# Two attentions of a diffusion block: a stage of their own, or woven head pair by head pair with linear layers

## The chip, the cores and the metric

One core of one Trainium2 chip runs the whole program. The metric is the device time of one execution in microseconds; the kernel before took 3308.38 us (median of three runs, 3305.70 to 3311.96). The core has a matrix engine (PE, with its weight loads shown as PEld), a vector engine (DVE), a scalar engine (ACT), a general one (POOL) and a queue engine (SP) that issues most transfers. Each runs its own list of instructions in order and waits for the others by semaphores. PE alone multiplies matrices; its sums land in PSUM and are read from there by DVE or ACT.

## The reference, cut to what matters

The program is a small diffusion transformer in fp32: two layers on 512 latent and 256 context tokens, width 1024, then a third block. The change concerns layer 0. Its mixer runs a window attention (8 query heads of width 64, 2 key heads, blocks of 128 queries, keys of the block before, its own and the next one, and all 256 context keys), an attention of the context tokens on themselves, and beside them a gated linear recurrence (HGRN, 4 heads, two directions).

```python
def window_attention(q, k, v, k_ctx, v_ctx, sink):
    ...
    def block(i):
        qb = lax.dynamic_slice_in_dim(q, start, ATTN_BLOCK, axis=3)
        kb = lax.dynamic_slice_in_dim(kp, start, span, axis=2)
        s_lat = jnp.einsum('bkgqd,bksd->bkgqs', qb, kb) * scale
        s_lat = jnp.where(valid, s_lat, -jnp.inf)
        s_ctx = jnp.einsum('bkgqd,bkcd->bkgqc', qb, k_ctx) * scale
        p = jax.nn.softmax(jnp.concatenate([sink_col, s_lat, s_ctx], axis=-1), axis=-1)
        return p_lat @ v  +  p_ctx @ v_ctx           # two einsums

def first_block(...):
    m_lat = jnp.split((cond_lat @ mod_w[layer] + mod_b[layer])[:, None, :], 6, axis=-1)
    h_lat = modulate(rms_norm(x, norm_g[layer, 0]), m_lat[0], m_lat[1])
    y_ctx, y_lat = even_mixer(h_ctx, h_lat, even_w_in[j], even_w_out[j], ...)
    # even_mixer: p = split_parts(h_lat @ w_in); attention on a_q, a_k, a_v; recurrence on b_*
```

## The kernel before, in words

Every linear is summed in three passes: weights are split into a rounded `hi` part (ACT, a CAST) and a remainder `lo` (POOL), inputs likewise, and PE sums hi x hi, lo x hi and hi x lo. A weight tile of 128x2048 comes by a DMA of SP into one of two `stage` buffers. `linear` runs one layer as a stage of its own; `chain` yields the same work piece by piece, and `Woven(...).upto(place)` lets another loop pull it in up to a place. Places are counted in matmuls of 512 columns: a job such as `bf1` (forget gates of head 1) or `bqg1` (query and output gate) or `bi0` (inputs of heads 0 and 1) has 72 of them. Stages are blocks with a barrier of all engines at both ends.

Layer 0 runs in this order. (1) First loads, the norm of x with its modulation, and the linears `aq` and `akv`. The modulation vectors are sums on DVE over tiles of 512 KB (`sum_up`, L926: two sums for each of 24 tiles, in four buffers); `first_mods` makes the two tiles of a chunk of the norm, `norm_split` calls it for chunks 0 and 1 ahead of the root and for chunk c+2 behind chunk c. (2) Norm and rotation of the attention's q and k, woven with `bf0`, `bqg0`, `bi0`. (3) `attend("win", ...)`: 4 blocks of 8 heads. Per head PE makes the scores of 640 keys against `q_zero` (full height, with the other key head's half filled with zeros), DVE scales and masks them and takes the maximum, ACT exponentiates, PE transposes 5 blocks, ACT copies them, PE multiplies by the values; per block of 8 heads DVE divides and PE transposes back. Nothing else runs there. (4) `attend("ctxa", ...)`: the same with 256 keys, 2 blocks. (5) The HGRN recurrence, 8 jobs (head and direction), woven with `bf1`, `bqg1`, `bf2`, `bqg2`, `bi1`, `bf3`, `bqg3` (504 places); `begin_of` says at which place each job starts, and jobs 6 and 7 run behind the linears. Much later, in layer 1, the linear `rg` has 24 modulation sums beside it (`rest_of_layer_1`), through two buffers.

## Time and profile before

| | us |
|---|---|
| median of three runs | 3308.38 |
| the profiled execution | 3308.32 |
| its span, first to last instruction | 3306.5 |
| PE busy | 2964.5 (90%) |
| DVE / ACT / POOL busy | 1268.1 / 1000.6 / 996.8 |
| loads from memory | 264.42 MB, 81 GB/s over the span |

A busy PE is an engine that had work under way, and its waits are put down to the instruction that released it. The stages above lie at 0 to 157.6 us, 157.6 to 233.6, 236.4 to 341.1, 341.1 to 370.4 and 370.4 to 633.3 us.

### The profile page before, as it was taken

To read this page: it belongs to the slowest core of one execution; us is meant where nothing else is said; L and a number is where in the kernel's file an instruction comes from. 1 tells how busy PE (TensorE), PEld (TensorE's weight loads), DVE (VectorE), ACT (ScalarE), POOL (GpSimd) and SP (SyncE) were. 2 spreads that over 40 slices of the span, in tenths; PEclk is the share of its full clock that TensorE was granted. 3 is DMA by queue.
4 is the path that set the end of the run, shared out by engine and by line. 5 is a ranking of instruction groups with operands and counts; after the bars stand their busy time and mean duration, and the time that the engine had idled before them with its cause. 6 is when DMAs were issued, how large, how long until landed. Compare 5 with 4: busy or idle time off the path is not lost. (4 is left out here: it accounts for less than half of the span.)

```text
span 3306.5 us, 38877 instructions
## 1 busy us (share of the span) xinstructions
PE 2964.5 (90%) x15588; PEld 2407.3 (73%) x15588; DVE 1268.1 (38%) x1869; ACT 1000.6 (30%) x1471; POOL 996.8 (30%) x482
## 2 busy tenths in 40 slices
PE   2789888679999999889997898999899999999998
PEld 1678787558888888868744686788668777886686
DVE  7456555472145116132015606511163554203523
ACT  2235554213211211422103314222243333324432
POOL 0220232112223222634102233344244433342333
PEclk7899899689999999999998999999989999999999
DMA  5300110141133113422202424432211111021121
GB/s 194 107 26 1 45 39 14 77 140 51 59 128 125 63 61 137 140 83 89 80 10 100 181 89 171 153 109 81 85 57 46 39 39 39 26 102 58 48 93 64
DMA packets 48958, 268.52 MB, mean 81 GB/s; under 512 B 5552, under 2 KB 6832, under 8 KB 28592
## 3 DMA queue, kind: packets, MB, share of 16 engines
q1 hardware_dynamic: 48816, 266.54, 23.0%
q8 instruction: 100, 1.64, 0.2%
q14 instruction: 42, 0.34, 0.0%
HBM read 264.42 MB, written 2.10 MB: 81 GB/s over the span
## 5 line engine op out<-in xcount | busy, mean ns | idle before, releaser
L416 POOL TENSOR_TENSOR shared_w_lo<-stage,shared_w_hi 128x2048 fp32r<-128x2048 f32 (+1 forms) x127 | 554.3, 4365 | 1363.1 <-ACT shared_w_hi L389 1360.0
L557 POOL TENSOR_TENSOR shared_w_lo<-stage,shared_w_hi 128x512 fp32r<-128x512 f32 (+2 forms) x233 | 300.7, 1319 | 515.6 <-ACT shared_w_hi L549 513.9
L389 ACT CAST shared_w_hi<-stage 128x2048 fp32r<-128x2048 f32 (+1 forms) x127 | 224.5, 1768 | 506.8 <-PE f0o_acc L479 134.5
L479 PE MATMUL f0i_acc<-norm_b_hi,shared_w_hi 128*128 128x512 f32 (+1 forms) x672 | 174.2, 341 | 2.0 <-PEq L368 2.0
L479 PE MATMUL f0i_acc<-norm_b_lo,shared_w_hi 128*128 128x512 f32 (+1 forms) x672 | 172.2, 337 | 0.0
L624 PE MATMUL two_acc<-norm_f_hi,shared_w_hi 128*128 128x512 f32 (+1 forms) x312 | 131.8, 422 | 9.1 <-DVE norm_f_lo L727 9.1
L549 ACT CAST shared_w_hi<-stage 128x1024 fp32r<-128x1024 f32 (+2 forms) x117 | 114.6, 1022 | 82.5 <-PE last_acc L624 43.9
L819 DVE TENSOR_TENSOR ffn_hidden<-f0i_acc,ffn_gate 128x512 f32<-128x512 f32 (+1 forms) x44 | 22.5, 553 | 301.0 <-PE f0i_acc L479 293.3
L479 PE MATMUL f1i_acc<-norm_e_hi,shared_w_hi 128*128 128x512 f32 x336 | 131.0, 390 | 2.3 <-PEq L368 1.6
L809 ACT CAST ffn_hi<-ffn_hidden 128x768 f32 (+3 forms) x44 | 32.0, 728 | 329.8 <-DVE ffn_hidden L819 329.8
L479 PE MATMUL f1i_acc<-norm_e_lo,shared_w_hi 128*128 128x512 f32 x336 | 130.8, 389 | 0.0
L624 PE MATMUL two_acc<-norm_f_lo,shared_w_hi 128*128 128x512 f32 (+1 forms) x312 | 129.9, 416 | 0.6 <-DVE dn_g_cum L2521 0.6
L479 PE MATMUL f0i_acc<-norm_b_hi,shared_w_lo 128*128 128x512 f32 (+1 forms) x672 | 124.5, 338 | 0.0
L479 PEld LDWEIGHTS f0i_acc<-norm_b_hi,shared_w_hi 128*128 128x128 f32 x672 | 102.7, 189 | 17.3 <-issue 2.3
L479 PEld LDWEIGHTS f0i_acc<-norm_b_lo,shared_w_hi 128*128 128x128 f32 x672 | 103.5, 189 | 15.6
L479 PEld LDWEIGHTS f0i_acc<-norm_b_hi,shared_w_lo 128*128 128x128 f32 x672 | 102.3, 188 | 15.1
L624 PE MATMUL last_acc<-norm_f_hi,shared_w_hi 128*128 128x512 f32 x256 | 102.6, 401 | 2.7 <-PEq L2431 1.8
L624 PE MATMUL last_acc<-norm_f_lo,shared_w_hi 128*128 128x512 f32 x256 | 102.0, 399 | 0.0
L479 PE MATMUL f0o_acc<-ffn_hi,shared_w_hi 128*128 128x512 f32 x352 | 92.2, 343 | 6.9 <-PEq L368 6.9
L624 PE MATMUL two_acc<-norm_f_hi,shared_w_lo 128*128 128x512 f32 (+1 forms) x312 | 92.1, 421 | 3.9 <-POOL shared_w_lo L557 3.9
L2206 DVE TENSOR_TENSOR ret_decayed<-ret_p_scores,ret_decay 128x512 f32<-128x512 f32 x24 | 16.5, 691 | 200.2 <-PE ret_p_scores L2179 100.8
L2646 POOL TENSOR_TENSOR delta_join<-delta_low,levels 128x512 f32<-128x512 f32 x56 | 72.4, 1303 | 65.7 <-PE delta_p L2688 38.4
(588 smaller groups left out, 7044.4 us busy)
## 6 DMA issues: line engine op xcount, KB each, us to landing
stage<-in_w_f0i SPq DMA_DIRECT2D x22, 1024.0 KB, 4.9
stage<-in_w_f1i SPq DMA_DIRECT2D x22, 1024.0 KB, 4.8
stage<-in_w_rv SPq DMA_DIRECT2D x16, 1024.0 KB, 4.8
mod_slots_a<-in_w_mod SPq DMA_DIRECT2D x24, 512.0 KB, 4.8
stage<-in_w_rqk SPq DMA_DIRECT2D x12, 1024.0 KB, 4.9
mod_slots_f<-in_w_mod SPq DMA_DIRECT2D x24, 512.0 KB, 4.0
mod_slots_e<-in_w_mod SPq DMA_DIRECT2D x24, 512.0 KB, 5.4
stage<-in_w_dqkv SPq DMA_DIRECT2D x12, 1024.0 KB, 4.9
```

The lines of the kernel that those rows point to most:

```text
L389: nc.scalar.copy(w_hi[:, slot, 0:size], stage[:, slot, 0:size]).then_inc(hi_ready, 1)
L416: nc.gpsimd.tensor_tensor(w_lo[:, slot, 0:size], stage[:, slot, 0:size], w_hi[:, slot, 0:size].bitcast(F32), ALU.subtract)\
L479: mm = nc.tensor.matmul(out[0:min(P, nt), b, 0:m], w[:, k, unit[1]:unit[1] + min(P, nt)], x[:, k, s:s + m], start=begin, stop=end)
L549: last = nc.scalar.copy(w_hi[:, index % 2, part], stage[:, index % 2, part])
L557: last = nc.gpsimd.tensor_tensor(w_lo[:, index % 2, part], stage[:, index % 2, part], w_hi[:, index % 2, part].bitcast(F32), ALU.subtract)
L624: mm = nc.tensor.matmul(out[0:min(P, nt), 0:m], weights[:, k, unit[1]:unit[1] + min(P, nt)], x[:, k, s:s + m], start=begin, stop=last)
L809: nc.scalar.copy(h_hi[:, bass.ds(t, 1), :], hidden[:].rearrange("p (o n) -> p o n", o=1))\
L819: last = nc.vector.tensor_tensor(hidden[:, s:s + m], res[1][:, b, 0:m], gate[:, s:s + m], ALU.mult)
L2206: nc.vector.tensor_tensor(decayed[:, n % 3, :], p_scores[:, n % 2, :], table[:, h % 2, at:at + LAT], ALU.mult).then_inc(rs["decayed"], 1)
L2646: nc.gpsimd.tensor_tensor(chunks(join[a][:]), chunks(low[a][:]), over_chunks(levels[:, m, :]), ALU.mult).then_inc(d["join"], 1)
```

## The change

`attend` is gone. One stage holds both attentions, unrolled into 24 pairs of heads (one head of each key head; 16 pairs of the window attention, 8 of the context's), woven with `bi0`, `bf1` and `bqg1`; the head-norm stage keeps `bf0` and `bqg0`, and the HGRN stage `bi1` and heads 2 and 3 (360 places). Queries and keys are used at half height (64 rows) without zeros; the keys are `k_rot` without padding, so that blocks 0 and 3 have 4 key blocks and not 5. The probabilities are divided before they are transposed, and the values are the stationary side, 64 columns wide, so that nothing is turned back. Each pair's scores are made one pair ahead. `begin_of` is new. In the first stage two modulation tiles are asked for ahead of x, the other twelve ahead of the next weight tile, chunks 0 to 3 are summed ahead of the root, and the first CAST stands behind the squares. Beside `rg` stand three sums per tile in place of four on six tiles.

```diff
-                        scales(dve, 0)
-                        scales(dve, 1)
+        SCALES_AHEAD = 4
+                        for c in range(SCALES_AHEAD):
+                            scales(dve, c)
 ...
-            return made["beside"]([0] * 8, [4] * 6 + [0, 0], scale_ffn_1)
+            return made["beside"]([0] * 8, [3] * 8, scale_ffn_1)
 ...
+                first_mod["load"](sp, 0)
+                first_mod["load"](sp, 1)
                 sp.dma_start(ones[:], io["ones"]).then_inc(loaded, 16)
                 sp.dma_start(x_lat[:], io["x"]).then_inc(loaded, 16)
 ...
-        def attend(tag, blocks, heads, q_copies, out_copies, width, kb_max, cols_out, scale, lse=None):
 ...
+            line_w = chain([input_job(0)] + head_jobs(1), acc_w, ahead=True)
+            weights_of = [2 if m < 16 else 1 for m in range(PAIRS)] + [1, 1]
 ...
+                    def scores(m):                       # PE
+                        i, c = divmod(m, 4)
+                        wait(pe, aw["scores_read"], 2 * m)
 ...
+                            for g in range(2):
+                                product(p_scores[g][:, 0:last - first], g, first, last)
+                            product(p_ctx[:, 0:CTX], 0, LAT, TOK).then_inc(aw["lat_scores"], 1)
+                            pe.wait_ge(aw["lat_scores"], m + 1)
+                            product(p_ctx[:, CTX:2 * CTX], 1, LAT, TOK).then_inc(aw["scores"], 2)
 ...
+                    scores(0)
+                    for m in range(PAIRS + 2):
+                        more.upto(pair_place(m))
+                        if m + 1 < PAIRS:
+                            scores(m + 1)
+                        if 1 <= m <= PAIRS:
+                            turn(2 * m - 2)
+                            more.upto((pair_place(m) + pair_place(m + 1)) / 2)
+                            turn(2 * m - 1)
+                        if m >= 2:
+                            mix_values(m - 2)
+                    more.rest()
 ...
+                    for m in range(PAIRS + 1):           # DVE
+                        for g in range(2):
+                            if m < PAIRS:
+                                read_scores(2 * m + g)
+                        more.upto(pair_place(m))
+                        for g in range(2):
+                            if m >= 1:
+                                normalize(2 * m - 2 + g)
+                        for g in range(2):
+                            if m < PAIRS:
+                                maximum(2 * m + g)
 ...
+                    for m in range(PAIRS + 2):           # ACT
+                        if 1 <= m <= PAIRS:
+                            copy_turned(2 * m - 2)
+                            copy_turned(2 * m - 1)
+                        if m < PAIRS:
+                            exponent(2 * m)
+                            exponent(2 * m + 1)
+                        if m >= 2:
+                            copy_out(m - 2)
+                        more.upto(pair_place(m))
 ...
-            line0 = chain(head_jobs(1) + head_jobs(2) + head_jobs(3), acc1, ahead=True)
+            line0 = chain([input_job(1)] + head_jobs(2) + head_jobs(3), acc1, ahead=True)
-            begin_of = [60, 130, 200, start_of["bqg2"][0] + 54, start_of["bf3"][0] + 2, start_of["bqg3"][0] + 10] + [after] * 3
+            begin_of = [56, 100, 160, start_of["bqg2"][0] + 56, start_of["bf3"][0] + 24, start_of["bqg3"][0] + 22] + [after] * 3
```

On PE, inside the window attention, this stood before: one head after the other, and nothing between (`turned` are the transposes, `mixed` the products with the values).

```order
L1167 MATMUL win_p_scores<-k_pad,q_zero 128x384
L1167 MATMUL win_p_scores<-k_pad,q_zero 128x256
L1176 MATMUL win_p_turned<-ident,win_row 128x128 x5
L1188 MATMUL win_p_mixed<-v_pad,win_probs 128x64 x5
L1167 MATMUL win_p_scores<-k_pad,q_zero 128x384
L1167 MATMUL win_p_scores<-k_pad,q_zero 128x256
```

And this stands there now, for one pair of heads (L630 are the sums of the linear `bf1`):

```order
L1408 MATMUL attend_scores<-k_rot,qk 128x384 x2
L1408 MATMUL attend_ctx_scores<-k_rot,qk 128x256 x2
L1428 MATMUL attend_turned<-ident,attend_row 128x128 x5
L630 MATMUL attend_acc<-norm_a_lo,shared_w_hi 128x384
L630 MATMUL attend_acc<-norm_a_hi,shared_w_hi 128x384
L630 MATMUL attend_acc<-norm_a_lo,shared_w_hi 128x384
L630 MATMUL attend_acc<-norm_a_hi,shared_w_hi 128x384
L630 MATMUL attend_acc<-norm_a_lo,shared_w_hi 128x384
L630 MATMUL attend_acc<-norm_a_hi,shared_w_hi 128x384
L1428 MATMUL attend_turned<-ident,attend_row 128x128 x5
L1439 MATMUL attend_mixed<-attend_probs,v_att 64x128 x10
```

The scores in it are those of the next pair, the transposes those of this pair and the products with the values those of the pair before; some six to eight matmuls of a linear stand at each of two places.

On DVE, at the same place of the program, one pair of heads is now this (`hgrn_i` is the reading of a sum of `bi0`); before, each head was the mask, the scaling, the sink column and the maximum, and the division came once in 8 heads:

```order
L1471 SCALAR_TENSOR_TENSOR attend_row<-attend_scores,window 128x384 [waits attend_turned,attend_scores]
L1474 TENSOR_SCALAR attend_row<-attend_ctx_scores 128x256
L1476 COPY attend_row<-small 128x1
L1210 COPY hgrn_i_980<-attend_acc 128x256 [waits unit_summed]
L1486 RECIPROCAL attend_inverse<-attend_total 128x1 [waits attend_exp]
L1490 TENSOR_SCALAR attend_row<-attend_row,attend_inverse 128x640 [waits attend_reciprocal]
L1486 RECIPROCAL attend_inverse<-attend_total 128x1 [waits attend_exp]
L1490 TENSOR_SCALAR attend_row<-attend_row,attend_inverse 128x640 [waits attend_reciprocal]
L1481 TENSOR_REDUCE attend_minus_max<-attend_row 128x1 [waits attend_scores_read] x2
```

The division works on the pair before, so that it stands between the reading and the maxima of this one, and the reading of a linear's sum stands ahead of both.

## Rows read from the trace of the kernel before

**Rows 1.** Busy time by stage: us, PE, PEld, DVE, ACT, POOL, clock, DMA share, GB/s
```profile
0.00:157.60 157.60, 80.21 (x416) 65.22 (x416) 93.05 (x145) 35.10 (x57) 18.82 (x8) 0.82 0.42 151
157.60:233.60 76.00, 67.47 (x366) 60.35 (x366) 41.44 (x36) 24.72 (x34) 28.38 (x26) 0.93 0.12 42
236.40:341.10 104.70, 94.77 (x624) 79.20 (x624) 59.51 (x136) 57.92 (x109) 0.00 (x0) 0.96 0.00 1
341.10:370.40 29.30, 23.89 (x136) 18.69 (x136) 16.02 (x52) 17.62 (x54) 0.00 (x0) 0.85 0.00 1
370.40:565.00 194.60, 169.94 (x1339) 158.69 (x1340) 106.31 (x160) 95.22 (x121) 65.22 (x42) 0.95 0.12 41
565.00:633.30 68.30, 37.23 (x280) 30.40 (x278) 31.94 (x45) 15.49 (x23) 3.57 (x2) 0.59 0.00 1
```

**Rows 2.** The same columns for the first transfers
```profile
4.00:24.00 20.00, 0.00 (x0) 0.00 (x0) 7.58 (x13) 3.61 (x2) 0.00 (x0) 1.00 1.00 413
```

**Rows 3.** DVE in order of time: start us, us, engine, line, op, count [idle before]
```profile
16.13 1.29 DVE L926 CUSTOM_DVE_ANT_0 mod_product_a<-mod_slots_a,conds_a,small 128x1024 f32<-128x1024 f32 x1 [16.13 <-DMA mod_slots_a<-in_w_mod]
...
24.92 5.26 DVE L926 CUSTOM_DVE_ANT_0 mod_product_a<-mod_slots_a,conds_a,small 128x1024 f32<-128x1024 f32 x1
...
38.35 4.95 DVE L721 RECIPROCAL norm_rstd<-norm_rstd 128x768 f32<-128x768 f32 x1 [6.36 <-ACT norm_rstd L694]
...
82.37 0.74 DVE L739 SCALAR_TENSOR_TENSOR norm_squares<-x_lat_in,scale_of,norm_rstd 128x512 f32<-128x512 f32 x1
...
90.39 0.74 DVE L739 SCALAR_TENSOR_TENSOR norm_squares<-x_lat_in,scale_of,norm_rstd 128x512 f32<-128x512 f32 x1
```

**Rows 4.** Group by form, head-norm stage: busy us, mean ns, idle before
```profile
L624 PE MATMUL head_acc<-norm_a_hi,shared_w_hi 128*128 128x384 f32 x64 | 24.0, 374 | 15.5 <-PEq L368 10.3 <-DVEq L1365 4.1 <-DVEq L1385 1.1
```

**Rows 5.** PE in order of time, one head of the window attention
```profile
274.61 1.30 PE L1167 MATMUL win_p_scores<-k_pad,q_zero 128*128 x4
275.74 0.71 PE L1176 MATMUL win_p_turned<-ident,win_row 128*128 128x128 f32 x5
276.29 1.23 PE L1188 MATMUL win_p_mixed<-v_pad,win_probs 128*128 x10
```

**Rows 6.** Groups by form, window attention (32 heads)
```profile
L1242 DVE TENSOR_REDUCE win_minus_max<-win_row 128x1 f32<-128x641 f32 x32 | 26.3, 821 | 1.1
...
L1236 DVE SCALAR_TENSOR_TENSOR win_row<-win_p_scores,window 128x384 f32<-128x384 f32 x32 | 17.6, 550 | 0.0
L1233 DVE TENSOR_SCALAR win_row<-win_p_scores 128x256 f32<-128x256 f32 x32 | 13.3, 416 | 0.0
```

**Rows 7.** DVE in order of time, a TENSOR_SCALAR in memory of 768 columns
```profile
374.18 0.68 DVE L1775 TENSOR_SCALAR hgrn_forget<-hgrn_forget,hgrn_bound 128x768 f32<-128x768 f32 x1 [5.31 <-DMA hgrn_restart<-in_restart]
```

**Rows 8.** PE in order of time, HGRN products at the end of the linears
```profile
568.74 0.66 PE L2007 MATMUL hgrn_p_out<-hgrn_scores,hgrn_i 128*128 128x128 f32 x4
...
571.34 0.87 PE L1979 MATMUL hgrn_p_scores<-hgrn_q_ref,hgrn_k_ref 128*32 128x64 f32 x48
572.14 1.16 PE L1994 MATMUL hgrn_p_kv<-hgrn_i,hgrn_k_end_tok 64*128 64x128 f32 x16
```

**Rows 9.** PE in order of time, half-height products and the linear behind them
```profile
423.76 0.71 PE L1994 MATMUL hgrn_p_kv<-hgrn_i,hgrn_k_end_tok 64*128 64x128 f32 x6
424.40 0.45 PE L624 MATMUL hgrn_acc<-norm_a_lo,shared_w_hi 128*128 128x384 f32 x1
424.68 0.34 PE L624 MATMUL hgrn_acc<-norm_a_hi,shared_w_hi 128*128 128x384 f32 x1
...
425.90 0.33 PE L624 MATMUL hgrn_acc<-norm_a_lo,shared_w_hi 128*128 128x384 f32 x1
```

**Rows 10.** Waits of PE from 370.4 to 633.3: us in total, times, longest
```profile
PE hgrn_p_scores L1979 <- DVE hgrn_q_cum L1796: 8.4, 5, 2.6
```

**Rows 11.** Queue of SP in order of time, the rg linear
```profile
1829.49 13.33 SPq L910 DMA_DIRECT2D mod_slots_f<-in_w_mod  x4
...
1843.98 13.29 SPq L910 DMA_DIRECT2D mod_slots_f<-in_w_mod  x4
```

More of the change, by code:

```diff
@@ L389, in round_hi @@
                             nc.scalar.copy(w_hi[:, slot, 0:size], stage[:, slot, 0:size]).then_inc(hi_ready, 1)
-                        if not begun:
-                            round_hi(0, 0)
-                        if made:
-                            made["act"](act)
+                        if side is not None and "sp_first" in side:
+                            made["act"](act, lambda: round_hi(0, 0))
+                        else:
+                            if not begun:
+                                round_hi(0, 0)
+                            if made:
+                                made["act"](act)
                         def body(t, j, last):
```

334 lines of the change are left out of this document (126 added, 208 removed).

## The prediction, as put on record before the change was run

> **What bounds the kernel now.** I read the table by stage first, then each stage's order of time, then groups and waits. The profiled execution took 3308.32 us, its span 3306.5, so 1.8 us lie outside it; the median of the runs is 3308.38, and sums made against the profile hold for it without correction. The table [rows 1] shows which stages a weave can fill. In the window attention PE is busy 94.77 of 104.7 us, in the context's 23.89 of 29.3, in the HGRN stage 169.94 of 194.6 as long as it has linears, then 37.23 of 68.3. So PE is the bound nearly everywhere in layer 0, also in the attentions, where DVE has 59.5 and ACT 57.9 us of 104.7. Hiding linears in PE's idle time alone can win some 15 us there. A larger gain has to come from less work of PE, so I count PE's work per pair of heads. The first stage is another case: PE 80 of 157.6 us, and DVE sets the pace with its modulation sums.
>
> **First stage.** Transfers run at 413 GB/s [rows 2]. Ahead of the first modulation tile stood x, context and ones, 3.2 MB or 7.8 us, which now come behind; the first sum moves from 16.1 us [rows 3] to about 8.4. But DVE has 16 sums to make now ahead of the root, 1.45 us each with their read-out, and only 4 buffers. Tile 4 is queued behind 8.7 MB and lands at about 26 us; the 8 sums on tiles 4 to 7 then last to 38. POOL's subtraction for the first weight tile, now later, falls among them. One sum took 5.26 us in place of 1.29 [rows 3], which costs 4 us and did before, so the reciprocal starts at 42 and not at 38.35. That the root itself is ready 6 us sooner, its CAST being gone from ahead of the squares, is then worth nothing. Behind it two chunks fewer carry sums: 52.0 us from the reciprocal to chunk 6 (38.35 to 90.39) less 2 x 5.8 is 40.4, so chunk 6 at 82.4 in place of 90.4. Eight us, of which I keep 7, as PE closes up over the last chunks. Bounds: 0 if the transfers queue worse, -12 if POOL's stall falls into a wait. The weight tile of `akv`, asked for behind all twelve loads now, is needed only 40 us later.
>
> **Head-norm stage.** `bi0` goes: 72 places. A place costs 0.232 us: seven matmuls of 384 columns in 1.22 us are 0.174 each, by 512/384 [rows 9]. That is 16.7 us. The chain of reciprocals on DVE (4.95 us each for 768 columns, as the one in [rows 3]; 5 chunks, with the rest of a chunk about 7.3 us) is 37 us long and fits into the remaining 59. PE waited 5.2 us for DVE's readings here, 10.3 more at the start [rows 4]. What gets worse is the end: silu of `bqg0` on ACT, a table load and two passes over 768 columns, some 3 us, stood beside `bi0` and now stands ahead of the barrier. Taken: -15, bounds -20 and -8.
>
> **Attention stage.** It replaces 136.8 us (233.6 to 370.4) and takes in 216 places, 50.1 us. PE's price of a pair of heads, five key blocks:
> - Scores. A head cost 1.13 us for 640 columns [rows 5], two cost 2.26. Half-height products may run side by side. The trace has such: 16 instructions of half-height 128 columns took 1.16 us, against 0.66 for only 4 at full height, 0.073 and 0.165 us each [rows 8]. The two masked parts then cost 1.1 us, and the two context parts, the second of which waits for the first, 0.9 with a wait of 0.1, less an overlap of 0.2 and rounded down: 1.8.
> - Transposes as before, 2 x 0.55 [rows 5].
> - Values. 1.23 us busy per head became 20 instructions of 128 columns in two column halves; at 0.073 that is 1.45, at the closer packing of the 128x32 products, 48 in 0.87 us [rows 8], far less. Taken: 1.3 for the pair.
> - Changes of form. Six half-height instructions took 0.71 us, and the first linear matmul behind them stood 0.28 us before the next, where 0.174 is usual [rows 9]: about 0.1 us a change, four a pair: 0.4.
> Sum 4.6, and 10.3 places of linears, 2.4: 7.0 us. Blocks 0 and 3 have four key blocks: scores 1.5, transposes 0.9, values 1.05, changes 0.4, linears 2.4: 6.25. DVE has per head 0.82 + 0.55 + 0.42 [rows 6], 0.15 for the sink, 0.3 for a reciprocal with its wait and 0.57 for the division (0.68 for 768 columns [rows 7]), 2.8, or 5.6 to 6.0 a pair with readings of sums. ACT has 57.92 / 32 = 1.8 a head [rows 1]. Both stay under 7.0, and the loop transpose, copy, exponential, division, transpose (0.55 + 0.7 + 1.0 + 0.9) has 4 us of other PE work beside it. A context pair is 3.3 us on PE and 3.6 on DVE, so 3.6. In all 8 x 7.0 + 8 x 6.25 + 8 x 3.6 = 135, 4 for the first pair, in which nothing overlaps, and 5 for the last two with the silu behind: 144, or +7 against 136.8, with 50 us of linears in it. Bounds: -10 (no price for the changes, context pairs PE-bound, no end) and +45. The latter is PE without anything side by side: 2.26 + 1.1 + 2.2 + 0.4 + 2.4 = 8.4, 7.3 and 4.3 a pair, 160 us, with the same ends and 10 of table loads and POOL against DVE.
>
> The half-height row is the nearest to the scores, so I go by it. The Trainium skill, TensorEngine Tiling (Array Packing), section Tiling Modes, says that changing the tiling mode drains the engine, which speaks against this change: 24 pairs go four times from one form to another. The trace shows a price of about 0.1 us for such a change [rows 9], 10 us in all; a full drain of the 0.3 us that one matmul takes there would make it 29 and the total about 3283. The same page, Restrictions and Gotchas, says that row tiles can't write the same PSUM bank at once, which would be why the second context part waits. No row here has that wait.
>
> **HGRN stage.** 144 places leave: -33.4 us. The eight jobs stay, and those inside the linears stand 44, 60, 40, 40, 70 and 64 places apart instead of 70, 70, 70, 92, 80 and 76. A job has 9 us of places and 8 to 11 of its own matmuls at 40, against some 11.5 us on DVE and in every second job 7 more for its norm. That is level with PE, and PE waited for the scaled queries 5 times already [rows 10]. I give back 8: -25, bounds -33 and -5. The tail of 68.3 us [rows 1] stays.
>
> **Beside rg.** Loads and sums of four modulation tiles held the queue 14.49 us (1829.49 to 1843.98 [rows 11]), with the next weight tile behind them; PE needs 48 x 0.232 = 11.1 a tile. Three take 10.9. Six tiles lost up to 3.4 each, 20 in all; I take half, as the first come early and the last two caught up. At the end three sums now stand behind the last reading, 5 to 6 us: -4, bounds -10 and +3.
>
> **Sum.** -7 - 15 + 7 - 25 - 4 = -44: 3308.3 - 44 = 3264.
>
> **Rivals.** (A) PE's halves don't run side by side between full-height work. Attention +45 in place of +7 less the 10 of contention: 3293 to 3302, say 3297. Against it stand the HGRN rows, which are taken between linears. (B) HGRN jobs are too dense. DVE's order (exponents of the next job ahead of this one's mask, the norm ahead of the next queries) makes PE wait in each of the six intervals by 4 more: -5 in that stage, 3284. For it: DVE would be 18.5 of 20 us busy at 40 places. (C) Slower: lock-step of the pairs. If scores, reading, division, maximum, exponential and transposes of a pair follow one another, since PE's linears stand in order behind a blocked transpose, a window pair takes 1.8 + 2.2 + 1.8 + 1.6 + 2.0 + 1.2 = 10.6, a context pair 5.5: 170 + 44 + 9 = 223 us, +86, and the total is 3343. It decides from about 188 us for the stage, 8.9 us a window pair. Against it: scores come a pair ahead, and rows have four slots. (D) Nothing moves: the linears taken in cost there what they cost before and PE's waits only change places, 3305. That needs A and B together.
>
> **How the numbers follow.** Forecast 0.66, B 0.13, A 0.12, D 0.03, C 0.06. Within the forecast the terms leave +-20. The range 3234 to 3298 holds the forecast, B and half of A. A measurement tells 0.2%, 6.6 us. Faster: forecast, B and nearly all of A, 0.91; same 0.03; slower 0.06.
>
> **What would show it.** The stage with the attentions lasts about 144 us, PE over 90% busy; a window pair comes every 7 us; the two scores' instructions of a pair start beside each other and one pair's take 1.8 us. The head-norm stage lasts 61 us, the HGRN stage up to its last linear 170, chunk 6 of the first norm starts at 82, `rg` is 4 us shorter. Window pairs above 8.9 us, or waits of PE for the division, would prove me wrong.

## The result and the profile after

The changed kernel took 3269.23 us (median of four runs, 3262.18 to 3279.86), the kernel before in the same runs 3309.64; the ratio is 0.9888, with a 95% interval of 0.9858 to 0.9918, about 37 us less. The forecast was 3264, the range 3234 to 3298. The profiled execution is the fastest of the four, 3262.18 us with a span of 3260.4. It is set against the span of 3306.5 before, 46 us less.

The page's line of busy times: PE's busy time is 36 us less in all (2964.5 before). 22.5 us of it lie in the stages of layer 0 (the windows below against those of the kernel before), where score products and products with values now use half the array each, two at a time. Another 7.6 lie beside `rg`, where the same matmuls ran at a higher granted clock (told under `rg_old`).

```profile
PE 2928.1 (90%) x15516; PEld 2363.9 (73%) x15516; DVE 1280.6 (39%) x1952; ACT 989.3 (30%) x1478; POOL 991.1 (30%) x478
```

The table of the windows by stage, to be read against [rows 1] (us, then busy us and instructions of PE, PEld, DVE, ACT and POOL, clock, DMA share, GB/s). A stage here begins with its first matmul; the attention stage is cut where the context's pairs begin, at 316.7.

```profile
0.00:148.50 148.50, 77.95 (x416) 63.61 (x417) 93.31 (x146) 35.22 (x58) 18.72 (x8) 0.83 0.44 160
148.50:209.40 60.90, 48.75 (x224) 41.41 (x224) 39.35 (x30) 23.01 (x33) 22.59 (x18) 0.91 0.10 35
209.40:316.70 107.30, 103.70 (x752) 80.77 (x752) 72.86 (x196) 48.16 (x106) 10.24 (x8) 0.95 0.09 30
316.70:364.60 47.90, 40.46 (x276) 28.16 (x275) 25.40 (x91) 28.55 (x76) 4.96 (x4) 0.92 0.00 1
364.60:533.00 168.40, 141.84 (x1134) 130.18 (x1134) 95.24 (x149) 83.84 (x111) 51.47 (x34) 0.90 0.10 35
533.00:607.40 74.40, 38.30 (x290) 31.61 (x290) 36.38 (x51) 19.12 (x28) 3.58 (x2) 0.63 0.02 5
```

With the same bounds the kernel before has 157.9, 79.9, 132.9, 191.5 and 73.5 us. What has to be seen: the head-norm stage lasts 60.9; the window part of the attention stage has PE busy 103.7 of 107.3 us; the context part of it is the poorer one, 40.5 of 47.9; the HGRN stage up to the last linear is 23 us shorter; its tail is as long as ever. The rest of the program follows with the same lengths, but for `rg` (122.6 us between the first matmuls of `rg` and `ro` before, 109.7 now) and about 5 us in later parts whose code is unchanged.

One window pair on PE, in order of time (pair 12, 256 masked columns; the `acc` rows are `bqg1`):

```profile
289.46 0.70 PE L1408 MATMUL attend_scores<-k_rot,qk 64*128 64x256 f32 x4
290.00 0.59 PE L1408 MATMUL attend_ctx_scores<-k_rot,qk 64*128 64x256 f32 x2
290.74 0.67 PE L1408 MATMUL attend_ctx_scores<-k_rot,qk 64*128 64x256 f32 x2
291.34 0.77 PE L1428 MATMUL attend_turned<-ident,attend_row 128*128 128x128 f32 x5
291.86 0.42 PE L630 MATMUL attend_acc<-norm_a_lo,shared_w_hi 128*128 128x384 f32 x1
292.12 0.34 PE L630 MATMUL attend_acc<-norm_a_hi,shared_w_hi 128*128 128x384 f32 x1
...
293.17 0.71 PE L1428 MATMUL attend_turned<-ident,attend_row 128*128 128x128 f32 x5
293.80 1.31 PE L1439 MATMUL attend_mixed<-attend_probs,v_att 128*64 128x128 f32 x20
295.05 0.44 PE L630 MATMUL attend_acc<-norm_a_hi,shared_w_hi 128*128 128x384 f32 x1
295.33 0.34 PE L630 MATMUL attend_acc<-norm_a_lo,shared_w_hi 128*128 128x384 f32 x1
```

The group of scores lasts 1.88 us (289.46 to 291.34). The four instructions of both masked parts, x4 in one row, start in twos 0.01 us apart, one of each head, and take 0.54 us up to the next row. One head's 256 columns alone would be 0.45, by the 1.13 us for 640 in [rows 5]: the two heads run side by side. The second context product starts 0.74 behind the first, though its own columns are 0.45; 0.3 is the wait for the first. Twenty products with the values take 1.25 us, what ten took for one head. The first linear matmul behind transposes or values stands 0.26 to 0.28 before the next, where 0.17 is usual [rows 9]; how much of that is a change of form is told in the section after the experiments.

The start of the context part, ACT first, then PE:

```profile
321.86 1.28 ACT L1182 ACT_TABLE_LOAD   x1
323.15 1.49 ACT L1182 ACTIVATE hgrn_forget<-hgrn_forget 128x1536 f32<-128x1536 f32 x1
324.55 1.97 ACT L555 CAST shared_w_hi<-stage 128x1024 fp32r<-128x1024 f32 x2
326.42 0.58 ACT L1520 COPY attend_probs<-attend_turned 128x512 f32<-128x512 f32 x1
```

```profile
327.15 1.08 PE L1428 MATMUL attend_turned<-ident,attend_row 128*128 128x128 f32 x4 [3.05 <-ACT attend_probs L1520]
328.16 1.98 PE L1439 MATMUL attend_mixed<-attend_probs,v_att 128*64 128x128 f32 x16
```

ACT loads the table for the sigmoid of `bf1`, works through 1536 columns, rounds a weight tile (`CAST`) and only then copies the transposed probabilities that PE's next transposes wait for. PE stands 3.05 us; the transposes behind take 1.0 where 0.5 is usual, since the granted clock is at the lower of its two levels (0.5, 1.2 GHz) for some 6 us from there. This pair lasts 9.6 us; in a run below where the stall is gone it lasts 5.0.

### The profile page after: what moved, and what is told of

Its sections match the earlier page's. It is cut to its first block and busy times, and to the rows that moved or that the text cites. A ratio compares the mean times of both kernels' runs of the same rounds, so it can differ in the third digit from the quotient of the medians.

```text
span 3260.4 us, 38562 instructions
## 1 busy us (share of the span) xinstructions
PE 2928.1 (90%) x15516; PEld 2363.9 (73%) x15516; DVE 1280.6 (39%) x1952; ACT 989.3 (30%) x1478; POOL 991.1 (30%) x478
## 5 line engine op out<-in xcount | busy, mean ns | idle before, releaser
L630 PE MATMUL two_acc<-norm_f_hi,shared_w_hi 128*128 128x512 f32 (+1 forms) x312 | 131.8, 422 | 9.1 <-DVE norm_f_lo L736 9.1
L828 DVE TENSOR_TENSOR ffn_hidden<-f0i_acc,ffn_gate 128x512 f32<-128x512 f32 (+1 forms) x44 | 22.5, 553 | 296.1 <-PE f0i_acc L485 288.5
L630 PE MATMUL two_acc<-norm_f_lo,shared_w_hi 128*128 128x512 f32 (+1 forms) x312 | 130.0, 417 | 0.6 <-DVE dn_g_cum L2465 0.6
L485 PEld LDWEIGHTS f0i_acc<-norm_b_hi,shared_w_lo 128*128 128x128 f32 x672 | 101.9, 188 | 14.6
L630 PE MATMUL last_acc<-norm_f_hi,shared_w_hi 128*128 128x512 f32 x256 | 102.6, 401 | 2.7 <-PEq L2375 1.8
L630 PE MATMUL last_acc<-norm_f_lo,shared_w_hi 128*128 128x512 f32 x256 | 102.0, 399 | 0.0
L630 PE MATMUL two_acc<-norm_f_hi,shared_w_lo 128*128 128x512 f32 (+1 forms) x312 | 90.6, 415 | 4.0 <-POOL shared_w_lo L563 4.0
L485 PE MATMUL f0o_acc<-ffn_lo,shared_w_hi 128*128 128x512 f32 x352 | 92.5, 344 | 0.0
```

What stands on the lines that cost most here:

```text
L485: mm = nc.tensor.matmul(out[0:min(P, nt), b, 0:m], w[:, k, unit[1]:unit[1] + min(P, nt)], x[:, k, s:s + m], start=begin, stop=end)
L630: mm = nc.tensor.matmul(out[0:min(P, nt), 0:m], weights[:, k, unit[1]:unit[1] + min(P, nt)], x[:, k, s:s + m], start=begin, stop=last)
L828: last = nc.vector.tensor_tensor(hidden[:, s:s + m], res[1][:, b, 0:m], gate[:, s:s + m], ALU.mult)
```

## The experiments

Stage lengths are between first matmuls. "Attention" goes from the first score product to the first linear of the HGRN stage; before, with both attentions and without linears, it was 132.9. Ratios are to the kernel before, with 95% intervals; `again`, `crossed`, `serial` and `apart` ran on one chip, `banked`, `sig_early`, `rg_old` and `b_first` on one, `sig_late`, `best` and `hg_wide` on one, `split` by itself.

| run | median us | before there | ratio | attention us |
|---|---|---|---|---|
| again | 3270.62 | 3300.21 | 0.9889 (0.9848 to 0.9930) | 154.1 |
| crossed | 3254.01 | 3300.21 | 0.9845 (0.9814 to 0.9877) | 145.0 |
| serial | 3299.78 | 3300.21 | 0.9989 (0.9972 to 1.0006) | 180.8 |
| apart | 3298.18 | 3300.21 | 0.9992 (0.9972 to 1.0013) | 179.2 |
| banked | 3253.32 | 3311.72 | 0.9824 (0.9804 to 0.9845) | 142.9 |
| sig_early | 3266.90 | 3311.72 | 0.9856 (0.9837 to 0.9876) | 152.8 |
| rg_old | 3285.68 | 3311.72 | 0.9913 (0.9893 to 0.9932) | 154.1 |
| b_first | 3299.36 | 3311.72 | 0.9959 (0.9937 to 0.9980) | 132.8 |
| sig_late | 3250.85 | 3302.68 | 0.9852 (0.9809 to 0.9896) | 140.0 |
| best | 3261.38 | 3302.68 | 0.9872 (0.9845 to 0.9899) | 140.0 |
| hg_wide | 3272.70 | 3302.68 | 0.9911 (0.9884 to 0.9938) | 154.1 |
| split | 3254.89 | 3306.71 | 0.9831 (0.9805 to 0.9858) | 138.2 |

**again.** The changed kernel, no edit.

> The changed kernel once more, nothing edited, as the base on the same chip for the runs beside it. Its first runs lay between 3262 and 3280 us. If the stages in the trace come out within 1 us of the first trace (148.5, 60.9, 155.2 and 242.8 us for the first, head-norm, attention and HGRN stages), differences of the stages between traces of a few us are real, and the spread of the totals comes from elsewhere.

Measured: stages of 148.5, 61.8, 154.1 and 248.5 us. The first three agree within 1.1, but the HGRN stage doesn't: its tail lasted 80.3 us against 74.4. So a difference of 2 us can be read from a trace up to the last linear of HGRN, while the totals spread by 20 us (3257 to 3277 here). What the tail does is told at the end.

**crossed.**

```diff
-                            for g in range(2):
-                                product(p_scores[g][:, 0:last - first], g, first, last)
-                            product(p_ctx[:, 0:CTX], 0, LAT, TOK).then_inc(aw["lat_scores"], 1)
-                            pe.wait_ge(aw["lat_scores"], m + 1)
-                            product(p_ctx[:, CTX:2 * CTX], 1, LAT, TOK).then_inc(aw["scores"], 2)
+                            product(p_scores[0][:, 0:last - first], 0, first, last)
+                            product(p_ctx[:, CTX:2 * CTX], 1, LAT, TOK).then_inc(aw["lat_scores"], 1)
+                            product(p_scores[1][:, 0:last - first], 1, first, last).then_inc(aw["scores"], 1)
+                            pe.wait_ge(aw["lat_scores"], m + 1)
+                            product(p_ctx[:, 0:CTX], 0, LAT, TOK).then_inc(aw["scores"], 1)
```

> Changed kernel, but the four score products of a window pair are issued crossed: masked part of head 0, context part of head 1, masked part of head 1, context part of head 0, with the wait on the first context part ahead of the last product. Theory (products on different row halves run side by side, if they go to different PSUM banks): both halves have 640 columns, so that the group takes 1.1 to 1.3 us in place of 1.88 to 2.09, about 0.8 us less a window pair, 16 pairs, attention stage 155 to about 143 us and the total 10 to 12 us less. Rival (halves don't run side by side; the 1.88 is something else): the group stays at 1.9 to 2.3 us and the stage at 155.

Measured: the group takes 1.61 us in blocks 1 and 2 and 1.40 in blocks 0 and 3, 0.48 less each. PE in order of time, the group of pair 12:

```profile
283.47 0.48 PE L1408 MATMUL attend_scores<-k_rot,qk 64*128 64x256 f32 x1
283.48 0.48 PE L1408 MATMUL attend_ctx_scores<-k_rot,qk 64*128 64x256 f32 x1
283.79 0.38 PE L1408 MATMUL attend_scores<-k_rot,qk 64*128 64x256 f32 x1
283.80 0.38 PE L1408 MATMUL attend_ctx_scores<-k_rot,qk 64*128 64x256 f32 x1
284.01 0.59 PE L1408 MATMUL attend_scores<-k_rot,qk 64*128 64x256 f32 x2
284.24 0.70 PE L1408 MATMUL attend_ctx_scores<-k_rot,qk 64*128 64x256 f32 x2
284.87 0.77 PE L1428 MATMUL attend_turned<-ident,attend_row 128*128 128x128 f32 x5
```

Each product is two instructions. Those of the first two products start in twos, one of each head, 0.01 us apart. Of the last two products only one instruction of each runs beside the other: the context product of head 0 starts 0.23 us behind the masked one of head 1. The attention stage lost 9 to 10 us (the theory had 12), the total 16, so that the halves do run side by side; the rival would have left the group as it was. The group did not come down to the 1.1 to 1.3 of the theory: the wait still stands in it.

**serial.**

```diff
-                            for g in range(2):
-                                product(p_scores[g][:, 0:last - first], g, first, last)
-                            product(p_ctx[:, 0:CTX], 0, LAT, TOK).then_inc(aw["lat_scores"], 1)
-                            pe.wait_ge(aw["lat_scores"], m + 1)
+                            product(p_scores[0][:, 0:last - first], 0, first, last).then_inc(aw["lat_scores"], 1)
+                            pe.wait_ge(aw["lat_scores"], 3 * m + 1)
 ...
```

> Changed kernel with a wait for the end of each score product ahead of the next one in the window pairs, so that nothing of them can run side by side. Theory (side by side): the group takes 2 x 1.13 us plus three waits of about 0.1, some 2.5 to 2.7 in place of 1.88 to 2.09; 16 pairs, the stage is 9 to 12 us longer and so is the total. Rival (nothing ran side by side before): only the two more waits are paid, 0.2 us a pair, stage and total +3.

Measured: 2.95 and 3.38 us a group. PE in order of time, the same kind of pair as above:

```profile
309.29 1.45 PE L1408 MATMUL attend_scores<-k_rot,qk 64*128 64x256 f32 x4
310.80 1.51 PE L1408 MATMUL attend_ctx_scores<-k_rot,qk 64*128 64x256 f32 x4
312.24 0.76 PE L1430 MATMUL attend_turned<-ident,attend_row 128*128 128x128 f32 x5
```

Four products of 256 columns are 1.8 us one after the other; 2.95 leaves 0.38 for each of the three waits (3.38 and 2.26 give 0.37), not the 0.1 that I had put. Some of that is the two changes of form at the group's ends. Read instruction by instruction, the wait behind a masked product costs 0.32 us (0.43 and 0.32 between starts where 0.22 is usual) and the one between the context products 0.38 (0.53 and 0.29). The stage became 26 us longer, in place of 9 to 12. 19 are 16 groups at 1.07 to 1.29 more; the other 7 or so lie in pairs at whose transposes and linears the granted clock was at its lower level (0.92 on average over the stage, 0.96 in `again`). The 19 hold two things that this run can't part by itself: two more waits in each group, 10 us at 0.32 each, and the lost overlap, which leaves 9 (an estimate). So products were side by side, and waiting for a product's end is as dear as going without the overlap. With both, nothing of the whole change is left (0.9989).

**apart.**

```diff
-                return line_w["end"] * sum(weights_of[:m]) / sum(weights_of)
+                return 0 if m <= PAIRS + 1 else line_w["end"]
```

> Changed kernel, but no linear matmul stands between the attention pairs: all 216 places of bi0, bf1 and bqg1 come behind the last pair, in the same stage. It tells what the weaving gives beside the new form of the attention. Theory 1 (the weave hides the pair's loop of transpose, copy, exponential and division): without linears a window pair costs 4.6 us on PE but DVE needs 5.6 to 6, so 16 x 5.8 + 8 x 3.6 + 5 = 127, then 50 us of linears: 177, +22 on the stage and the total. Theory 2 (the gain is in PE's own work, half-height products, not in the weave): the pairs come at PE's pace of 4.4, stage 155 as with the weave, total unchanged. Lock-step would show as pairs of over 8 us: stage over 200.

Measured: the stage is 179.2 us (177 by theory 1), the total 28 more than `again`. PE in order of time, one pair:

```profile
274.28 0.92 PE L1408 MATMUL attend_scores<-k_rot,qk 64*128 64x384 f32 x4
...
276.37 0.77 PE L1428 MATMUL attend_turned<-ident,attend_row 128*128 128x128 f32 x5
278.01 0.74 PE L1428 MATMUL attend_turned<-ident,attend_row 128*128 128x128 f32 x5 [0.87 <-ACT attend_probs L1520]
278.68 1.31 PE L1439 MATMUL attend_mixed<-attend_probs,v_att 128*64 128x128 f32 x20
279.92 0.49 PE L1408 MATMUL attend_scores<-k_rot,qk 64*128 64x256 f32 x2
```

A pair comes every 5.64 us (274.28 to 279.92), of which PE's own work is 4.4 (2.09 of scores, 2 x 0.55 of transposes, 1.24 of values): the second head's transposes start 1.64 behind the first head's, since they wait 0.87 for ACT's copy to free the PSUM they write. Theory 1 had the length of the stage right and its cause wrong: DVE, on which it put 5.6 to 6 us a pair, is busy for 4.70 of the 5.64. At the end stand 52 us of linears alone. With linears between, the same pair costs 7.2, so that its 2.7 us of them cost only 1.6 more. That is 1.1 us won a pair, 18 over 16. A context pair costs 2.95 without and 3.27 with its 1.5 us of linears, 9 over eight. The stage shows 24 to 25 of these 27. The weave alone is thus worth 25 us, and without it too the whole change is worth nothing (0.9992).

**banked.** As `crossed`, and in blocks 0 and 3:

```diff
+                            if len(near) == 2:
+                                for g in range(2):
+                                    product(p_scores[g][:, 0:2 * P], g, first, last)
+                                for g in range(2):
+                                    product(p_scores[g][:, 2 * P:2 * P + CTX], g, LAT, TOK).then_inc(aw["scores"], 1)
+                                return
```

> Changed kernel; in blocks 1 and 2 the score products are issued crossed as in the run before, and in blocks 0 and 3, where the masked part has only 256 columns, each head's context part goes behind it into the same PSUM bank, so that no product waits for another. Theory (the rest of the group is side by side, and a wait for the end of a product costs 0.37 us, as the run with three waits gave: 3.38 less 2.26 for three): the group takes 1.61 us in blocks 1 and 2 as crossed, and 2 x 0.43 = 0.9 in blocks 0 and 3, where it was 1.88 in the changed kernel and 1.40 crossed; attention stage 155.2 - 8 x 0.5 - 8 x 1.0 = 143, total 12 to 20 us below the changed kernel. Rival (DVE, or the loop of a pair, takes over once PE's pair falls below 6.4 us, as PE without linears came every 5.64): PE waits at the transposes in blocks 0 and 3 and the stage stays near the 145.0 of the crossed run.

Measured: 1.06 us a group in most pairs of blocks 0 and 3, without a wait in it (PE in order of time, the next fence; the theory had 0.9, the columns alone), 1.61 in the others, the stage 142.9 for 143; DVE and the loop of the pair did not take over, though a pair is down to 6.2.

```profile
281.36 1.14 PE L1408 MATMUL attend_scores<-k_rot,qk 64*128 64x256 f32 x8
282.42 0.77 PE L1434 MATMUL attend_turned<-ident,attend_row 128*128 128x128 f32 x5
```

**sig_early.**

```diff
                 if u == 3:
-                    yield 8
+                    yield 0 if h == 1 else 8
```

> Changed kernel; ACT takes the sigmoid of bf1 (table load, 1536 columns, and the load back) one pair earlier, among window pairs of 7 us and not at the first context pair. In both traces of the changed kernel the pair there lasts 9.2 to 9.6 us in place of about 3.9, with PE's clock at half for some us behind it. Theory (ACT's 4 us of table loads and sigmoid with 2 us of cast stand ahead of the copy that PE waits for): the pair falls to about 4.5, one window pair rises by 0 to 2, stage 155 to 150 or 151, total -4 to -6. Rival (the same stall moves with the sigmoid, since a window pair has ACT 3.2 us busy and 6 more don't fit into 7): stage 153 to 156, total unchanged.

Measured: 152.8 us, 1.3 to 2.4 less. Pair 17 fell from 9.6 to 5.3, but pair 16, the one before it, rose from 5.4 to 7.2: PE waited 2.1 us there for ACT's copies. The truth is between the two, nearer to the rival; the total can't tell it.

**sig_late.** As `banked`, and the sigmoid taken out of the forget job of head 1 and put here:

```diff
+                if h == 1 and u == 1:
+                    yield 24
+                    act.wait_ge(gla_sem["raw"], 12)
+                    nc.scalar.activation(keep[1][:], keep[1][:], ACT.Sigmoid).then_inc(gla_sem["sigmoid"], 1)
```

> The run with crossed and banked scores, and in it the sigmoid of bf1 on ACT behind the last exponential (24 pairs on), where the silu of bqg1 follows and no exponential comes back. Theory (two table loads, the sigmoid and a cast in one string ahead of the copy are the whole of the stall): the pair at the start of the context attention falls from 9.1 to 3.9 us, nothing is paid at the end, since PE has 7 us of work there, and the attention stage is 142.9 - 5 = 138. Rival (moved stall, as one pair earlier, where 1.8 us of PE's wait stayed in the last window pair and the stage fell by 1.3 to 2.4 only): the end of the stage is 3 to 4 us later and the stage 141 to 143.

Measured: pair 17 lasts 4.97 us (9.07 in `banked`), the stage 140.0, between the theory's 138 and the rival's 141 to 143. The 4 us of the stall are gone, and one of them comes back at the end, where PE now stands 4.0 us and not 2.7 (in the changed kernel) while sigmoid and silu together hold the barrier. So the order of ACT was the cause of that stall; the pair is still 1.1 us above the 3.9 of the theory.

**best.** As `sig_late`, with another row of counts.

```diff
-            return made["beside"]([0] * 8, [3] * 8, scale_ffn_1)
+            return made["beside"]([0] * 8, [4, 4, 3, 3, 3, 3, 2, 2], scale_ffn_1)
```

> The run before this with 4, 4, 3, 3, 3, 3, 2, 2 modulation sums per tile of rg in place of 3 each. In the changed kernel PE waits 9.9 us for the first inputs of ro behind rg, 6.4 more than in the kernel before, since three sums stand behind the last reading. Theory (each sum there costs what it lasts with its load, about 2.2 us, and the first tile has PE's 10 us wait to hide one more): ro's wait falls to about 7.5, and the stretch stays at 110: total -2. Rival (the second tile's fourth sum holds the next weight tile up, as in the kernel before): the stretch grows by 3, total +1.

Measured: PE's wait for `ro` fell from 9.7 to 6.4 us, but a wait of 3.0 for the next weight tile of `rg` appeared, and the stretch went from 109.9 to 111.5. That is the rival, at half its size. The profiled execution is 14.6 us longer than that of `sig_late`: 1.6 are this stretch; 6 lie in the HGRN tail and 9 behind `ro` (some 2 are less elsewhere), where the code is the same, and say nothing.

**rg_old.**

```diff
-            return made["beside"]([0] * 8, [3] * 8, scale_ffn_1)
+            return made["beside"]([0] * 8, [4] * 6 + [0, 0], scale_ffn_1)
```

> Changed kernel with the old counts beside rg: four modulation sums on six tiles and none on the last two. Theory (the whole of the rg stretch's gain, from 122.6 to 109.8 us between first matmuls of rg and ro, is due to these counts): the stretch is 122 to 123 us again and the total 12 to 13 us more. Rival (part of it is a clock effect or comes with the earlier stages): 113 to 119, total +4 to +9. My prediction had put 4 us on it.

Measured: the stretch is 126.9 us, 17 more than in the changed kernel (the theory had 12 to 13), and 4 more than before; the total is 19 above `sig_early` on the same chip. PE's waits in that stretch (us in total, times, longest), here:

```profile
PE rg_acc L485 <- DVE ret_qk L2187: 26.4, 6, 10.1
PE ro_acc L485 <- DVE mixed_lo L784: 3.5, 1, 3.5
```

and in the changed kernel:

```profile
PE rg_acc L485 <- DVE ret_qk L2187: 10.1, 1, 10.1
PE ro_acc L485 <- DVE mixed_lo L784: 9.9, 1, 9.9
```

Of PE's 26.4 us of waits, 16.3 go with three sums a tile, in which DVE and the queue keep up with PE's 11 us a tile. The wait behind the last tile grows from 3.5 to 9.9. So waits explain 9.9 of the 17.2 us. The rest is the clock (the stretch in `rg_old`, then in the changed kernel, columns as in [rows 1]):

```profile
1749.50:1876.40 126.90, 96.97 (x387) 77.00 (x385) 81.93 (x82) 29.86 (x31) 38.09 (x8) 0.91 0.43 150
1741.50:1851.20 109.70, 89.65 (x387) 73.26 (x385) 84.98 (x82) 29.33 (x31) 36.83 (x8) 0.93 0.51 174
```

The same 387 matmuls keep PE busy for 7.3 us less. In `rg_old` PE stands 1.6 to 6.9 us ahead of five more tiles, and at three of these waits (2.8, 3.4 and 6.9 us) the granted clock goes to its lower level (0.5, 1.2 GHz) for 3.4 to 6.8 us; in the changed kernel no such wait follows the first, and from 1766.8 to 1845.3 the clock is 1.00. So both sides of the run's question hold a part: the counts are the cause of all 17 us, and 7 of them come by the clock.

**b_first.** The kernel before with the diff's lines of the first stage (the two loads ahead of x, `sp_first`, `SCALES_AHEAD`, the CAST behind the squares).

> Kernel before with the first stage of the change alone (two modulation tiles asked for ahead of x, the other loads ahead of the next weight tile, four chunks summed ahead of the root, first CAST behind the squares). Theory: the first stage ends at 148.5 to 149.7 us in place of 157.9, all other stages as before, total -8 to -9 against the kernel before. Rival (the gain is given back at the barrier or in the next stage, whose first matmuls wait for weights): the head-norm stage is longer by some us, total -4 or less.

Measured (windows of the three first stages):

```profile
0.00:149.10 149.10, 79.15 (x417) 64.63 (x417) 93.55 (x146) 35.25 (x58) 19.86 (x10) 0.81 0.44 160
149.10:229.20 80.10, 66.63 (x366) 59.80 (x366) 42.17 (x36) 25.81 (x36) 28.18 (x25) 0.95 0.12 40
229.20:362.00 132.80, 117.45 (x761) 96.59 (x761) 75.31 (x188) 74.40 (x162) 0.00 (x0) 0.95 0.00 1
```

The first stage is 8.8 us shorter, and nothing is given back in the next two (80.1 and 132.8 for 79.9 and 132.9). The total is lower by 12, with an interval of 7 to 21 that holds 8.8.

**hg_wide.**

```diff
-            begin_of = [56, 100, 160, start_of["bqg2"][0] + 56, start_of["bf3"][0] + 24, start_of["bqg3"][0] + 22] + [after] * 3
+            begin_of = [56, 112, 172, start_of["bf3"][0] + 10, start_of["bqg3"][0] - 4, start_of["bqg3"][0] + 50] + [after] * 3
```

> Changed kernel with the HGRN jobs farther apart: they start at 56, 112, 172, 226, 284 and 338 in place of 56, 100, 160, 200, 240 and 310. Theory (at 40 places a job is level with PE, and PE's waits in the stage, 29 us in 168 against 24 in 191 before, come partly from that): PE waits 5 to 10 us less up to the last linear, which comes 3 to 8 us sooner, and the tail is longer by what of job 5 is left, 5 to 8: total within 4 us of the changed kernel. Rival (density costs nothing, the waits are the ends of norms and the start of the stage): the last linear stays at 168 and the total is 5 to 8 us more.

Measured (windows of the stage up to its last linear, and of the tail):

```profile
363.40:524.10 160.70, 134.88 (x1130) 124.02 (x1131) 92.55 (x146) 83.18 (x109) 52.31 (x34) 0.94 0.11 37
524.10:609.00 84.90, 47.49 (x297) 39.91 (x295) 40.17 (x54) 19.77 (x29) 3.58 (x2) 0.55 0.02 4
```

The last linear comes after 160.7 us in place of 168.4, the tail lasts 84.9 in place of 74.4 to 80.3. But the waits did not fall, as the theory wanted: PE waits 25.8 us up to the last linear, against 26.6 of 168.4 in the changed kernel. It is PE's busy time that is 7.0 less there, for four instructions fewer (141.84 (x1134) there), at a granted clock of 0.94 for 0.90; in the tail it is 9.2 more (47.49 for 38.30), at 0.55 for 0.63. So the first theory's length came by another cause, and spacing moves clock from one side to the other and wins nothing.

**split.** As `sig_late`, and in blocks 1 and 2:

```diff
+                            product(p_scores[0][:, 0:3 * P], 0, first, last)
+                            product(p_ctx[:, P:2 * P], 1, LAT + P, TOK).then_inc(aw["lat_scores"], 1)
+                            product(p_scores[1][:, 0:3 * P], 1, first, last)
+                            product(p_scores[0][:, 3 * P:4 * P], 0, LAT, LAT + P)
+                            pe.wait_ge(aw["lat_scores"], m + 1 - 4)
+                            product(p_ctx[:, 0:P], 0, LAT + P, TOK).then_inc(aw["scores"], 1)
+                            product(p_scores[1][:, 3 * P:4 * P], 1, LAT, LAT + P).then_inc(aw["scores"], 1)
```

> The run with the late sigmoid (crossed and banked scores), and in blocks 1 and 2 the context part of each head is cut in two: 128 columns go behind the masked part into the head's own bank, the other 128 into the shared one, and the one that another product waits for is issued early and is short. Each half height has 640 columns as before; DVE has one reading of 128 columns more a head. Theory (what is left of the 1.61 us group above the 1.1 of its columns is the wait for the end of a 256-column product): the group falls to 1.1 or 1.2, 8 pairs, attention stage 140.0 to 136 and total 3 to 4 us less. Rival (DVE's two readings more, 0.3 us each, or the loop of the pair holds PE): pairs stay at 6.6 to 6.8 and the stage at 139 to 141.

Measured: the group takes 1.41 us, 0.2 less and not 0.4 to 0.5; pairs follow it (6.4 to 6.6), and the stage is 138.2. Neither theory is met: DVE did not hold PE, but the group stayed 0.3 above its columns. 0.16 of that is no wait, since `banked` has it in the group that waits for nothing (1.06 for 0.9); the theory had taken it for a part of the wait. The rest, 0.1 to 0.15, is open.

`banked`, `sig_late` and `split` (ratios of 0.9824, 0.9852 and 0.9831) are clearly faster than the kernel before. Against the changed kernel's 0.9888 (0.9858 to 0.9918) only `banked` has an interval that lies wholly below; that of `split` touches it, and that of `sig_late` overlaps. They overlap one another too, so that the totals don't rank them: in `split` the stretch of `rg`, whose code is unchanged, lasts 114.3 us where it lasts 110 in the others. By the stage in the trace all three are 11 to 17 us shorter than the changed kernel, and `split` is the shortest.

## Why the prediction was right, point by point

The time was right to 5 us, the parts less so. Forecast and measured, stage by stage (traces of the changed kernel and of before):

| step | forecast | measured |
|---|---|---|
| first stage | -7 | -9.4; b_first alone -8.8 |
| head-norm stage | 61 long | 60.9 |
| attention stage | 144 long | 155.2, 154.1 |
| HGRN up to the last linear | 170 long | 168.4, 168.2 |
| HGRN tail | unchanged | +0.9, +6.8 |
| rg to ro | -4 | -12.9, -11.7 |

**First stage.** Right by its steps. DVE in order of time:

```profile
9.47 1.29 DVE L935 CUSTOM_DVE_ANT_0 mod_product_a<-mod_slots_a,conds_a,small 128x1024 f32<-128x1024 f32 x1 [9.47 <-PEq L1103]
...
26.06 1.29 DVE L935 CUSTOM_DVE_ANT_0 mod_product_a<-mod_slots_a,conds_a,small 128x1024 f32<-128x1024 f32 x1 [1.53 <-DMA mod_slots_a<-in_w_mod]
...
31.97 5.09 DVE L935 CUSTOM_DVE_ANT_0 mod_product_a<-mod_slots_a,conds_a,small 128x1024 f32<-128x1024 f32 x1
...
41.67 4.94 DVE L730 RECIPROCAL norm_rstd<-norm_rstd 128x768 f32<-128x768 f32 x1
...
82.14 0.75 DVE L748 SCALAR_TENSOR_TENSOR norm_squares<-x_lat_in,scale_of,norm_rstd 128x512 f32<-128x512 f32 x1
```

The first sum stands at 9.47 (8.4 forecast). Tile 4 (the fifth, since they are counted from 0) is waited for until 26.06 (26 forecast); one sum behind it ran into POOL's work and took 5.09, and the reciprocal stands at 41.67 (42) in place of 38.35 [rows 3]. Chunk 6 stands at 82.14 (82.4). Only the 1 us kept back at the end was not needed: chunk 6 is 8.3 us earlier, and the stage ends 9.4 earlier.

**Head-norm stage.** Right: 60.9 for 61.

**Attention stage.** The forecast's +7 over the old length was mis-sized by 11, and the runs show where. The window part was right: in the middle a pair came every 6.7 to 7.3 us (7.0 forecast), at both ends every 5.4 to 7.0 (6.25), 107.3 us up to the first context pair for the 110 in the sum. Inside a pair, transposes (1.16 with the change of form), values (1.25 for 1.3) and linears with their changes (2.75 for 2.8) were as put. The scores were 2.09 and 1.88 for 1.8 and 1.5, and their two parts were off in opposite ways: both masked parts took 0.75 us for the 1.1 put, both context parts 1.34 for 0.9, since the wait between these costs 0.38 us for the 0.1 put and they don't overlap at all. The context part took 47.9 for 34. Three things make this up: ACT's sigmoid with its table loads (4 to 6 us, which I had kept in the upper bound, as "table loads", and left out of the value), the last window pairs' transposes and values, which fall among the first context pairs (1.8), and the last pair with what follows, 14.5 us from 350.1 on for the 8.6 put, since PE has two pairs' work and their linears to do when the last scores are made. The sign named as proof against the forecast, PE waiting for the division, does show in the context part, but only with 1.5 us in three waits; in the window part there is none.

**Changes of form.** The price of 0.1 us was misread from the row, and the sum didn't suffer by it. The 0.26 behind transposes is no change of form, since both are 128*128: the last transpose starts at 291.83 and the second linear matmul behind it at 292.12, which is one transpose (0.11) and one linear matmul (0.17). Behind the values it is otherwise. The last two value products, one of each column half, start here:

```profile
294.84 0.28 PE L1439 MATMUL attend_mixed<-attend_probs,v_att 128*64 128x128 f32 x2
```

The second linear matmul starts at 295.33, 0.48 us behind them in place of 0.28: a change back to full height and width costs 0.20. Half of it lies ahead of the first linear matmul, where the prediction did not look. Into the values (last transpose at 293.60, second two products at 293.96, 0.36 in place of 0.22) a change costs 0.14. With about 0.20 and 0.15 around the scores that is some 0.7 us a pair and not 0.4. The difference was in the group prices already, which the prediction took from rows that have such changes at their ends. The Trainium skill, TensorEngine Tiling (Array Packing), section Tiling Modes, lets a change of the tiling mode drain the engine. A price of 0.14 to 0.20 a change agrees with that; a drain of a whole matmul's 0.3 us did not show here. In the crossed run products of both halves that go to different PSUM banks start 0.01 us apart; with what the Trainium skill says on the same page, in Restrictions and Gotchas, of row tiles that write one bank, this agrees so far as it goes. No run here has two of them in one bank at the same time.

**HGRN stage.** -25 forecast, -22 measured, of which -23 up to the last linear. So 10 of the 33.4 us were given back, where I had put 8, and most of them not by the cause that I had named. PE waits 26.6 us in 168.4 there and had 23.0 in 191.5, so that denser jobs cost at most 3.6. PE's busy time fell from 168.50 to 141.84, 26.7 us and not 33.4: 6.7 are matmuls at the lower clock (0.90 granted on average, 0.95 before), for which the sum had no term. That the size fits is luck.

**Beside rg.** The term of -4 was mis-sized: -12.9. Its two parts were about right. The waits for weight tiles, 20 us that I had halved to 10, fell by 11.8 (21.9 before, 10.1 now; in `rg_old` 26.4), and the part at the end, 6 us, is 6.4 (9.9 for 3.5). What the sum left out is the clock behind the waits: PE's busy time in the stretch fell by 7.6 us (97.24 to 89.65).

**The sum.** -9.4 - 19.0 + 22.3 - 22.2 - 12.9 is -41 with the head-norm and attention stages counted from the same bounds, and -5 lies where no code changed. That too small a loss in one stage met too small a gain in another is why the total fits better than its terms, and that is luck.

**Rivals.** A (no products side by side) fell: `crossed` shows them side by side in the trace, and `serial`, which has A for the scores and two more waits a pair, costs 26 us in the stage. B (HGRN too dense) fell: it wanted some 20 us of waits more and there are 3.6, and with wider spacing they stay. C (lock-step) fell: window pairs of 7.0 to 7.3, not 10.6; even without linears between them they come every 5.64. D fell with A and B. Two of their sums were a few us off: A's 160 + 9 + 10 is 42 above 136.8 and not 45, and B's six intervals of 4 are 24 where its -5 allows for 20.

## What to carry to other kernels

Count the bounding engine's work per unit of the loop, and look then for what only some of the units meet: the weave was right to 0.3 us a pair in its steady part and wrong where a table switch, a change from long to short units and the emptying of the pipeline came. Two halves of the array help only if nothing between them waits: order the products so that the one waited for is issued early and is short, or give each its own bank. Work that switches ACT's function table belongs where no other function comes back soon. And where a wait of PE is taken away or made, count what the clock does behind it: beside `rg` that was 7 us on top of 10 of waits.

## What the runs showed of the hardware

A wait on PE for the end of its own product of 256 or 384 columns cost 0.32 to 0.38 us beyond the product (`serial`, instruction by instruction). Going from full-height linears or transposes to products on half the array or back cost 0.14 to 0.20 us a change (the changed kernel, pair 12).

The same program has a shorter and a longer HGRN tail, 74.4 and 80.3 us, by the clock granted in it. Windows of the first 10 us, of the changed kernel and then of `again`:

```profile
533.00:543.00 10.00, 7.30 (x66) 7.33 (x66) 6.39 (x8) 3.18 (x4) 0.00 (x0) 1.00 0.01 2
```

```profile
533.00:543.00 10.00, 7.65 (x41) 7.68 (x41) 6.05 (x8) 2.84 (x3) 0.00 (x0) 0.67 0.01 2
```

The clock (the column behind POOL) is 1.00 in one and 0.67 in the other, where both come out of the same linears. `apart` had the long tail too, `crossed` and `serial` the short one of 74.5. In that part PE is busy about half the time (38.3 of 74.4 us), and where its clock changes level is not the same in each run. The tail makes 6 of the 12 us by which the two profiled executions of the changed kernel differ (spans of 3260.4 and 3272.4), so that gains of 2 to 5 us are to be read from a stage and not from a total.
